# Products of no use in TensorE's waits inside the mLSTM recurrence of a two-block transformer step

## The chip, the cores and the metric

The kernel runs on one core of a Trainium2 chip. Its metric is the device time of one execution in microseconds (us), of which the median over several runs counts. TensorE's clock is granted at one of two levels, 1.2 and 2.4 GHz; in the profile 0.50 stands for the first and 1.00 for the second.

## The reference

Two transformer blocks are computed for 1024 tokens of width 1024, each with a mixer and a mixture of experts. The change touches one part of the first block: the mLSTM mixer, a recurrence over chunks of 128 tokens, run forward and backward, with four heads of 64 key and 128 value columns. For every chunk it needs the state left by the earlier chunks (`C_prev`) and the products inside the chunk:

```python
def _mlstm_chunk_outputs(q, k, v, log_i, log_f, prev):
    ...
    m_t = jnp.maximum(a, jnp.max(log_d, axis=-1))
    s = jnp.einsum('bhctk,bhcsk->bhcts', qc, kc) * jnp.exp(log_d - m_t[..., None])
    e_int = jnp.exp(a - m_t)
    num = (jnp.einsum('bhcts,bhcsv->bhctv', s, vc)
           + e_int[..., None] * jnp.einsum('bhcvk,bhctk->bhctv', C_prev, qc))
    den = jnp.sum(s, axis=-1) + e_int * jnp.einsum('bhck,bhctk->bhct', n_prev, qc)
    h = num / jnp.maximum(jnp.abs(den), jnp.exp(-m_t))[..., None]
```

## The kernel before

The program is a row of stages, each with its own instruction list for every engine; the engines meet only at semaphores. `stage_mlstm` holds the recurrence. Its unit of work is a pair, that is two heads of one direction in one chunk: 10 chunks (two of them context) by two directions by two pairs of heads make 40 pairs `p`. The first 8 belong to the context and give only a state; for the other 32, numbered `v` from 0, outputs are computed too. Two successive pairs, `v` even and `v` odd, are the four heads of one chunk and one direction. They share one set of decay factors, so one turn of the pattern is two pairs.

For a pair `v` TensorE does, in this order (lines of the kernel before):

- the inter product, queries by the state left by earlier chunks (L948), into columns 256 to 384 of two PSUM banks; the banks alternate with `v` (`out_banks`: banks 2 and 3, or 4 and 5);
- a wait until VectorE has finished the weights `pt` of this same pair `v` (`pt_ready`, v + 1);
- the scores of the next pair, keys by queries (L918), into banks 0 and 1;
- the value product, `pt` by the values (L954), into columns 0 to 128 of the same two banks as the inter product, with `start=True`, so that what stood there is overwritten;
- after an even `v`, the maxima for the next turn (L910), two products of 512 columns in the fp32r format;
- the local product, keys by weighted values (L966), from which VectorE makes the new state. It waits for GpSimd's `wv` and for VectorE to have read the one before.

VectorE does for each turn: `mask` (L1042, decay from the maxima), `weights` (L1051, `pt` = scores by decay) for the next pair, the sum of the inter and value products (L1063, `hsum`), four small operations for the denominator and the output (L1066 to L1077), and the new state (L1081). Beside them it has work of the convolution branch: a `reciprocal` of 128 columns for `v` 0 to 7 (L1090), and a product of 512 columns for `v` 12 to 19 (L1095). ScalarE exponentiates the decay factors, four operations ahead of odd `v`'s end (L977), scales the inter product (L995), squares finished outputs (L980), and takes one square root at `v` = 10 (L1005), with a change of activation table before and behind it. TensorE's order is the order in which the code is written; no planner is involved.

Of the kernel before, what the change touches and what calls it, by code (L numbers as in the profile page):

```python
# [31 lines left out]
KC = D_CONV // P  # L32
# [807 lines left out]
def stage_mlstm(s):  # L840
# [19 lines left out]
    with ExitStack() as stack:  # L860
# [5 lines left out]
        NM_high, NM_low = (sb(f"NM_{n}", [NCOL, P]) for n in ("high", "low"))  # L866
        NM4 = [sb(f"NM4_{n}", [NCOL, H1, P]) for n in ("high", "low")]
        R = lambda ap: ap.bitcast(F32R)
# [8 lines left out]
        out_banks = lambda v: 2 + 2 * (v % 2)  # L877

        with nc.Block() as block:
            @block.sync  # L880
            def _(sp):
                sp.wait_ge(zeros_set, 1)
                for i in range(2 * NT):
                    t, a = divmod(i, 2)
                    sp.dma_start(s.second_sum[t * P:(t + 1) * P, a * 512:(a + 1) * 512], zeros[:, :]).then_inc(zeros_stored, 16)
                sp.wait_ge(zeros_stored, 16 * 2 * NT)
# [18 lines left out]
            @block.tensor  # L905
            def _(pe):
                def maxima(g):

                    for i in range(2):
                        last = pe.matmul(s.bank[6].rearrange("p (h n) -> p h n", h=H1), R(group_of[:, NC * 2 + g:NC * 2 + g + 1]).to_broadcast([NCOL, P]),  # L910
                                         R(NM4[i][:, :, :]), start=(i == 0), stop=(i == 1))
                    last.then_inc(maxima_done, 1)

                def scores(v):
                    j, d, k = pairs[P0 + v]
                    t0 = tile_of(j, d) * P
                    for i in range(2):
                        last = pe.matmul(s.bank[i][:, 0:P], s.qkT[lanes(i), 2 + k, t0:t0 + P], s.qkT[lanes(i), k, t0:t0 + P],  # L918
                                         start=True, stop=True)
                    last.then_inc(scores_done, 1)  # L920

                for n, m in halves:
                    last = pe.matmul(s.bank[2 + n][:, :], s.ones[:, :], s.y[:, m, n * N:(n + 1) * N], start=(m == 0), stop=(m == KC - 1))
                    if m == KC - 1:
                        last.then_inc(mean_done, 1)
                for p, (j, d, k) in enumerate(pairs):
                    v = p - P0
                    if v in (-4, -3):
                        n = v + 4
                        for m in range(KC):  # L930
                            pe.wait_ge(squared, n * KC + m + 1)
                            last = pe.matmul(s.bank[4 + n][:, :], s.ones[:, :], sqy[:, m, n * N:(n + 1) * N], start=(m == 0), stop=(m == KC - 1))
                        last.then_inc(var_done, 1)
                    if v == 0:
                        pe.wait_ge(centred, 2 * KC)
                    if v == 1:
                        pe.wait_ge(var_read, 2)
                    if v == -1:
                        pe.wait_ge(maxima_set, 1)
                        maxima(0)  # L940
                        scores(0)
                    if v >= 0:
                        t0, bank = tile_of(j, d) * P, out_banks(v)
                        if v >= 2:
                            pe.wait_ge(combined, v - 1)
                        pe.wait_ge(state_moved, p - H1 + 1)
                        for i in range(2):
                            pe.matmul(s.bank[bank + i][:, 256:256 + W], s.qkT[lanes(i), k, t0:t0 + P], state[lanes(i), d, k, :],  # L948
                                      start=True, stop=True)
                        pe.wait_ge(pt_ready, v + 1)  # L950
                        if v + 1 < NV:
                            scores(v + 1)
                        for i in range(2):
                            last = pe.matmul(s.bank[bank + i][:, 0:W], pt[:, v % 2, i, :], s.v_aug[:, tile_of(j, d), 2 * k + i, :],  # L954
                                             start=True, stop=True)
                        last.then_inc(num_done, 1)
                        if v % 2 == 0 and v + 2 < NV:
                            pe.wait_ge(masked, v // 2 + 1)
                            maxima(v // 2 + 1)
                    if p < PS:  # L960
                        pe.wait_ge(wv_ready, 2 * (p + 1))
                        if p >= 1:
                            pe.wait_ge(state_moved, p)
                        for i in range(2):
                            h = 2 * k + i
                            last = pe.matmul(s.bank[7][lanes(i), 0:W], s.k_tok[:, tile_of(j, d), h * DK:(h + 1) * DK],  # L966
                                             wv[:, p % 2, i, :], start=True, stop=True)
                        last.then_inc(local_done, 1)
# [192 lines left out]
class OutNorm:  # L1161
# [47 lines left out]
    R = staticmethod(lambda ap: ap.bitcast(F32R))  # L1209
# [1535 lines left out]
class BlockEntry:  # L2745
# [44 lines left out]
    R = staticmethod(lambda ap: ap.bitcast(F32R))  # L2790
# [1360 lines left out]
```

## Time and profile before

| | us |
|---|---|
| median of 3 runs | 2859.05 |
| all runs | 2858.34, 2859.05, 2865.69 |
| the profiled execution | 2865.83 |
| its span, first to last instruction | 2864.1 |
| TensorE's mean granted clock over the span | 0.949 |
| TensorE busy | 2650.1 (93%) |
| VectorE busy | 1795.9 (63%) |
| ScalarE busy | 1294.6 (45%) |
| GpSimd busy | 1105.4 (39%) |

The recurrence proper, the 32 pairs with outputs, lies from about 423 us to 538 us after the span's start, 4% of it; most of the rest is the two expert stages. A matmul's busy time in this profile includes the time in which its last columns pass through the array, so matmuls that follow each other closely overlap: the distance from one start to the next is what one costs in a row. In a row of the timeline, "x4" means four instructions merged into one row, the number after the start is the time they take together, and the bracket at the end is the idle time of the engine ahead of them and what ended it. "issue" is idle time in which nothing that the profile shows was waited for.

### The profile page before, as it was taken

What the parts mean: (1) busy time and instruction counts of PE and PEld (TensorE: products, weight loads), DVE (VectorE), ACT (ScalarE), POOL (GpSimd) and SP (SyncE); (2) the same over time, 40 slices, a digit from 0 to 9 for tenths busy, and PEclk for the clock granted to TensorE, in tenths of its full rate; (3) what the DMA queues carried; (4) which work ended last, traced back from release to release, by engine and by line L of the source; (5) the groups of instructions that cost most, each with busy time, mean ns of one, the idle gap of its engine ahead of it and who ended that gap; (6) DMA issues with size and microseconds to landing.
All of it is one profiled execution on the core that took longest, in us unless ns stands there. A gap on an engine that the chain in (4) does not pass through costs nothing. (4 is left out here: it accounts for less than half of the span.)

```text
span 2864.1 us, 40780 instructions
## 1 busy us (share of the span) xinstructions
PE 2650.1 (93%) x12404; PEld 1987.1 (69%) x12405; DVE 1795.9 (63%) x2593; ACT 1294.6 (45%) x1816; POOL 1105.4 (39%) x1056
## 2 busy tenths in 40 slices
PE   6999989699899999999999977999999999877998
PEld 3455446486478888888888866875876877765786
DVE  3766767766677678678686657555544342557764
ACT  3320123632266567677675544146123232326653
POOL 1870023111666567567675540249201010005454
PEclk9999995699999999999999998999999999987999
DMA  8340010134288789999898866200311332428972
GB/s 296 133 154 1 30 59 1 68 128 187 82 305 294 249 291 323 306 328 316 265 353 296 259 162 207 73 1 2 62 45 52 103 88 66 171 110 312 323 225 43
DMA packets 187315, 484.59 MB, mean 169 GB/s; under 512 B 37484, under 2 KB 93344, under 8 KB 166456
## 3 DMA queue, kind: packets, MB, share of 16 engines
q1 hardware_dynamic: 143072, 372.83, 35.1%
q0 software_dynamic: 42592, 106.04, 15.5%
q10 hardware_dynamic: 1544, 4.33, 0.4%
q8 instruction: 62, 1.02, 0.2%
q14 instruction: 45, 0.37, 0.0%
HBM read 432.35 MB, written 95.69 MB: 184 GB/s over the span
## 5 line engine op out<-in xcount | busy, mean ns | idle before, releaser
L2219 PE MATMUL psum<-moe_high,moe_xg_high 128*128 128x512 f32 x960 | 390.0, 406 | 16.8 <-issue 16.7
L2221 PE MATMUL psum<-moe_high,moe_xg_low 128*128 128x512 f32 x960 | 378.0, 394 | 0.0
L2220 PE MATMUL psum<-moe_low,moe_xg_high 128*128 128x512 f32 x960 | 375.3, 391 | 0.0
L1633 DVE TENSOR_TENSOR moe_low<-moe_raw,moe_high 128x2048 fp32r<-128x2048 f32 x160 | 358.9, 2284 | 3.0 <-ACT moe_high L1617 1.5
L1617 ACT ACTIVATE moe_high<-moe_raw 128x2048 fp32r<-128x2048 f32 x160 | 297.9, 1920 | 11.0 <-DMA moe_raw<-in_w_e_up 8.3
L1609 POOL DMA_INDIRECT moe_landing<-moe_rows,moe_ig_now x124 | 225.9, 1822 | 109.4 <-POOL moe_ig_now L1606 91.4
L1606 POOL COPY moe_ig_now<-idx 128x1 int32 (+1 forms) x124 | 172.9, 1394 | 198.4 <-DVE moe_xg L1646 158.9
L2219 PEld LDWEIGHTS psum<-moe_high,moe_xg_high 128*128 128x128 f32 x960 | 181.7, 189 | 54.7 <-issue 20.5
L2206 PE MATMUL psum<-moe_high_down,moe_hid_high 128*128 x488 | 203.6, 417 | 8.9 <-DVE moe_hid_low L2297 8.6
L2221 PEld LDWEIGHTS psum<-moe_high,moe_xg_low 128*128 128x128 f32 x960 | 180.8, 188 | 42.9
L2220 PEld LDWEIGHTS psum<-moe_low,moe_xg_high 128*128 128x128 f32 x960 | 181.9, 190 | 36.0
L2252 ACT ACTIVATE moe_y_blk<-psum,row_w 128x1024 f32 x124 | 138.4, 1116 | 131.0 <-PE psum L2208 112.5
L2208 PE MATMUL psum<-moe_high_down,moe_hid_low 128*128 x488 | 192.2, 394 | 0.0
L2207 PE MATMUL psum<-moe_low,moe_hid_high 128*128 x488 | 192.1, 394 | 0.0
L590 DVE SCALAR_TENSOR_TENSOR conv_y<-upad,convw,conv_y 128x1024 f32<-128x1024 f32 x120 | 182.4, 1520 | 5.9 <-DVE x L621 1.7
L1633 DVE TENSOR_TENSOR moe_low<-moe_raw,moe_high_down 128x2048 fp32r<-128x2048 f32 x80 | 182.7, 2283 | 0.0
L1661 DVE TENSOR_TENSOR moe_xg_low<-psum,moe_xg_high 128x512 fp32r<-128x512 f32 x244 | 157.3, 686 | 27.0 <-ACT moe_xg_high L1656 26.5
L567 PE MATMUL psum<-hT,w_ring 128*128 128x512 f32 x384 | 169.0, 598 | 1.1 <-PEq L200 1.1
L2263 ACT ACTIVATE moe_silu<-psum 128x256 f32<-128x256 f32 x120 | 46.0, 383 | 272.7 <-PE psum L2221 272.7
L2302 DVE TENSOR_TENSOR moe_hid<-psum,moe_silu 128x256 f32<-128x256 f32 x120 | 50.4, 420 | 182.0 <-ACT moe_silu L2263 181.2
L1622 ACT ACTIVATE moe_high_down<-moe_raw 128x2048 fp32r<-128x2048 f32 x80 | 153.2, 1916 | 3.4 <-DMA moe_raw<-in_we_down 2.0
L1656 ACT ACTIVATE moe_xg_high<-psum 128x512 fp32r<-128x512 f32 x244 | 132.9, 597 | 15.1 <-PE psum L1650 8.9
(635 smaller groups left out, 5695.2 us busy)
## 6 DMA issues: line engine op xcount, KB each, us to landing
moe_raw<-in_we_gate SPq DMA_DIRECT2D x64, 1024.0 KB, 8.9
moe_raw<-in_we_up SPq DMA_DIRECT2D x64, 1024.0 KB, 12.6
moe_raw<-in_we_down SPq DMA_DIRECT2D x64, 1024.0 KB, 8.9
x<-in_w_ada POOLq DMA_DIRECT2D x16, 1024.0 KB, 5.6
x<-in_w_in SPq DMA_DIRECT2D x32, 512.0 KB, 6.4
moe_raw<-in_w_e_gate SPq DMA_DIRECT2D x16, 1024.0 KB, 9.6
moe_raw<-in_w_e_up SPq DMA_DIRECT2D x16, 1024.0 KB, 13.1
moe_raw<-in_w_e_down SPq DMA_DIRECT2D x16, 1024.0 KB, 9.9
```

Source lines behind the costliest of these rows:

```text
L567: last = pe.matmul(bank[:, 0:width], w[:, k, c0:c0 + P], h[:, k, :], start=(k == 0), stop=(k == KD - 1))
L590: c.link(dve, dve.scalar_tensor_tensor(to, rows, w, to, ALU.mult, ALU.add))
L1606: pool.tensor_copy(self.ig_now[q][:, :], idx[:, bass.ds(g + 2, 1)]).then_inc(self.ig_set, 1)
L1609: pool.indirect_dma_start(self.landing[:, q * D:(q + 1) * D], None, self.rows, bass.IndirectOffsetOnAxis(ap=self.ig_now[q][:, 0:1], axis=0 ...
L1617: act.activation(self.high[:, at:at + 2048].bitcast(F32R), self.raw[r][:, part], ACT.Copy).then_inc(self.w_high, 1)
L1633: dve.tensor_tensor(self.low[:, at:at + 2048].bitcast(F32R), self.raw[r][:, part], hi, ALU.subtract).then_inc(self.w_low, 1)
L2206: pe.matmul(by[n][:, :], R(hid_high[:, f, :]), w_hi, start=(f == 0), stop=False)
L2207: pe.matmul(by[n][:, :], R(hid_high[:, f, :]), w_lo, start=False, stop=False)
L2208: last = pe.matmul(by[n][:, :], R(hid_low[:, f, :]), w_hi, start=False, stop=(f == KF - 1))
L2219: pe.matmul(to, x_hi, R(of_k(w_hi, k)), start=(k == 0), stop=False)
L2220: pe.matmul(to, x_hi, R(of_k(w_lo, k)), start=False, stop=False)
L2221: last = pe.matmul(to, x_lo, R(of_k(w_hi, k)), start=False, stop=(k == KD - 1))
```

## The change

A function `keep_running` issues 8 matmuls for each of the pairs `v` = 0 to 7 and 4 for each later one, 8 x 8 + 24 x 4 = 160 in all, each with its own weight load. They stand between the inter product and the wait for `pt`. Each multiplies the 80 x 128 array `NM_high` by 256 columns of the 80 x 512 array `NM4[0]` in fp32r and writes columns 0 to 255 of the first of the pair's two banks. Nobody reads the result: the value product of the same pair overwrites columns 0 to 128, and columns 129 to 255 are never read. The inter product's columns start at 256 and stay as they are. No semaphore is added.

```diff
+                def keep_running(v):
+
+                    for _ in range(8 if v < 2 * KC else 4):
+                        pe.matmul(s.bank[out_banks(v)][:, 0:256].rearrange("p (h n) -> p h n", h=2), R(NM_high[:, :]), R(NM4[0][:, 0:2, :]), start=True, stop=True)
+
...
                         for i in range(2):
                             pe.matmul(s.bank[bank + i][:, 256:256 + W], s.qkT[lanes(i), k, t0:t0 + P], state[lanes(i), d, k, :],
                                       start=True, stop=True)
+                        keep_running(v)
                         pe.wait_ge(pt_ready, v + 1)
                         if v + 1 < NV:
                             scores(v + 1)
```

TensorE's instructions at the start of the recurrence, from the local product ahead of pair 0 to the inter product of pair 1, in the kernel before (`c_state` is the state, `qkT` queries and keys, `wv` the weighted values; a row is a matmul as written, before its passes):

```order
L966 MATMUL psum<-wv,k_tok 64x129 x2
L948 MATMUL psum<-c_state,qkT 128x129 x2
L918 MATMUL psum<-qkT 128x128 x2
L954 MATMUL psum<-v_aug,pt 128x129 x2
L910 MATMUL psum<-NM_high,group_of 128x512
L910 MATMUL psum<-NM_low,group_of 128x512
```

The same place in the changed kernel, whose lines are numbered 5 and 6 higher:

```order
L972 MATMUL psum<-wv,k_tok 64x129 x2
L953 MATMUL psum<-c_state,qkT 128x129 x2
L917 MATMUL psum<-NM_high 128x256 x8
L923 MATMUL psum<-qkT 128x128 x2
L960 MATMUL psum<-v_aug,pt 128x129 x2
L910 MATMUL psum<-NM_high,group_of 128x512
L910 MATMUL psum<-NM_low,group_of 128x512
```

Between the inter product and the next pair's scores there are now eight matmuls of 256 columns; the rest keeps its order, and so does every other engine's list.

## Rows read from the trace of the kernel before

**Rows 1.** Stretches of the recurrence: busy time (instructions) by engine, granted clock, DMA share, GB/s.
```profile
423.00:433.00 10.00, 6.90 (x58) 4.66 (x56) 6.91 (x20) 3.81 (x13) 4.74 (x8) 1.00 0.00 1
433.00:515.00 82.00, 76.45 (x372) 52.23 (x371) 62.04 (x203) 32.86 (x107) 26.53 (x44) 0.50 0.00 1
515.00:533.00 18.00, 11.37 (x90) 7.69 (x89) 13.62 (x48) 9.97 (x42) 2.40 (x4) 0.97 0.01 1
533.00:545.00 12.00, 3.90 (x16) 2.88 (x16) 5.60 (x23) 8.85 (x38) 0.00 (x0) 0.50 0.00 1
```

**Rows 2.** Waits from 422 to 540: total us, times, longest.
```profile
ACT inter L995 <- PE psum L954: 16.9, 15, 1.4
...
DVE c_state L1081 <- PE psum L966: 4.3, 2, 3.6
```

**Rows 3.** VectorE's timeline: two turns, at 1.2 and at 2.4 GHz.
```profile
505.11 0.69 DVE L1042 TENSOR_TENSOR decay<-psum,neg_mask 128x512 f32<-128x512 f32 x1
506.55 0.42 DVE L1051 TENSOR_TENSOR pt<-psum,decay 128x256 f32<-128x256 f32 x1 [0.76 <-ACT decay L977]
507.64 0.43 DVE L1063 TENSOR_TENSOR hsum<-psum,inter 128x258 f32<-128x258 f32 x1 [0.67 <-ACT inter L995]
...
511.67 0.68 DVE L1042 TENSOR_TENSOR decay<-psum,neg_mask 128x512 f32<-128x512 f32 x1
...
518.35 0.68 DVE L1042 TENSOR_TENSOR decay<-psum,neg_mask 128x512 f32<-128x512 f32 x1
...
524.89 0.68 DVE L1042 TENSOR_TENSOR decay<-psum,neg_mask 128x512 f32<-128x512 f32 x1
```

**Rows 4.** TensorE's timeline at 1.2 GHz, a turn of the first eight pairs.
```profile
447.55 0.80 PE L918 MATMUL psum<-qkT 64*128 64x128 f32 x4 [0.77 <-DVE pt L1051]
448.28 1.23 PE L954 MATMUL psum<-v_aug,pt 128*128 128x129 f32 x4
...
455.44 0.80 PE L918 MATMUL psum<-qkT 64*128 64x128 f32 x4 [0.78 <-DVE pt L1051]
```

**Rows 5.** ScalarE's timeline around the square root of pair 10.
```profile
464.51 0.63 ACT L995 ACTIVATE inter<-psum,EI 128x129 f32<-128x129 f32 x2 [1.42 <-PE psum L954]
465.16 1.28 ACT L1005 ACT_TABLE_LOAD   x1
...
468.83 1.28 ACT L977 ACTIVATE decay<-decay,E 128x128 f32<-128x128 f32 x4
```

**Rows 6.** VectorE's timeline at the same place, and at pair 31.
```profile
469.55 0.42 DVE L1051 TENSOR_TENSOR pt<-psum,decay 128x256 f32<-128x256 f32 x1 [1.98 <-ACT decay L977]
...
537.69 0.43 DVE L1063 TENSOR_TENSOR hsum<-psum,inter 128x258 f32<-128x258 f32 x1 [0.27 <-ACT inter L995]
```

**Rows 7.** TensorE's timeline at 2.4 GHz: inter product, wait, scores, value product.
```profile
429.58 0.49 PE L948 MATMUL psum<-c_state,qkT 64*128 64x129 f32 x4
431.71 0.49 PE L918 MATMUL psum<-qkT 64*128 64x128 f32 x4 [1.63 <-DVE pt L1051]
...
525.49 0.49 PE L948 MATMUL psum<-c_state,qkT 64*128 64x129 f32 x4
526.81 0.49 PE L918 MATMUL psum<-qkT 64*128 64x128 f32 x4 [0.83 <-DVE pt L1051]
527.23 0.71 PE L954 MATMUL psum<-v_aug,pt 128*128 128x129 f32 x4
```

**Rows 8.** TensorE's timeline in the output projection: fp32r products of 512 columns.
```profile
569.57 0.60 PE L1259 MATMUL psum<-out_w_high,out_src_high 128*128 128x512 f32 x1 [4.76 <-DVE out_w_low L1432]
569.98 0.63 PE L1260 MATMUL psum<-out_w_low,out_src_high 128*128 128x512 f32 x1
...
573.32 0.39 PE L1259 MATMUL psum<-out_w_high,out_src_high 128*128 128x512 f32 x1
573.55 0.40 PE L1260 MATMUL psum<-out_w_low,out_src_high 128*128 128x512 f32 x1
```

**Rows 9.** One line's weight loads: count, ns min/median/max, first and last start, shape.
```profile
L3857 PEld LDWEIGHTS psum<-h_high,gw_high x256: 186/188/189, 2168.9 to 2432.3; 128*128 128x128 f32 x128
```

## The prediction

> **What bounds the kernel now.** I read the page first for where the recurrence lies and how large it is: 115 us of 2864. Then the stretches of that part, with the clock [rows 1]. TensorE's clock was granted at 2.4 GHz until 433 us, stood at 1.2 GHz from 433 to 515 us, rose, and fell again near 533 us. In the 82 us at 1.2 GHz TensorE was busy for 76.45 us, 93%; that looks like a stretch bounded by TensorE at half its clock, and if it were, giving the clock back would be worth tens of us. So the question is whether anybody waits for TensorE there.
>
> The waits answer it [rows 2]. VectorE waited for TensorE's local product 4.3 us, in two waits, one of them 3.6 us long, so it is nothing that comes back in every turn. ScalarE waited for the value product 16.9 us over 15 waits, but what counts is whether VectorE then waited for ScalarE because of it. VectorE's timeline shows a turn of two pairs [rows 3]: the mask, then 0.76 us idle until ScalarE has exponentiated enough of the decay factors, the weights, then 0.67 us idle until ScalarE's `inter` is there. That `inter` belongs to the odd pair; ScalarE runs it only behind its four exponentials, so it is late because of them and not because of a value product. Otherwise VectorE works without a break. The loop is VectorE's work plus those two waits for ScalarE, 1.43 us a turn, in which TensorE has no part.
>
> The trace holds a direct test. From mask to mask the turn at 1.2 GHz took 511.67 - 505.11 = 6.56 us, and the turn at 2.4 GHz took 524.89 - 518.35 = 6.54 us [rows 3], with the same work on VectorE. Twice the clock brought 0.02 us. The turn between the two, in which the clock rose, took 6.68 us, with no gain in it either.
>
> **The change part by part.** It adds 160 fp32r matmuls of 256 columns. It removes nothing and moves no other instruction, on any engine. It has two effects: they take TensorE's time, and they may hold the clock at 2.4 GHz.
>
> Price of one at 2.4 GHz. The trace has no fp32r product of 256 columns in the recurrence. The nearest row is of 512 columns: start to start 573.55 - 573.32 = 0.23 us [rows 8]. Columns stream at a constant rate, so I take half, 0.115 us; four are 0.46 us and eight 0.92 us. The upper end is 0.23 us, if the halved columns gain nothing because something else sets the pace: 0.92 and 1.84 us. The lower end is zero, which is what a product costs that is hidden whole.
>
> Weight loads. In a row of such products a weight load lasts 0.188 us [rows 9] though the products start 0.23 us apart, so it lies beside the product before it. The Trainium skill (TensorE: Matmul & The Clock Gate, Part 3, "What overlaps and what doesn't") says that weight loads overlap products in flight only when the row group differs, which speaks against this change, since all the added products use the same rows. This trace does not bear it out: the products of the projection share all 128 rows and still stand 0.23 us apart. By the rule one added product would cost some 0.115 + 0.188 = 0.30 us, eight 2.4 us; by the row it is 0.115 us.
>
> What hides them. Ahead of the scores of an even turn half, TensorE was idle at 2.4 GHz for 1.63 us in the first eight pairs and for 0.83 us in the later ones, until `pt` was there [rows 7]. In the odd half `pt` is ready and there is no such wait, so those products push TensorE's list back until the next wait takes them up. The two halves together bring 2 x 0.92 = 1.84 us against 1.63, and 2 x 0.46 = 0.92 against 0.83: TensorE would be 0.21 or 0.09 us late at the scores. That is covered too. The scores and value product took 448.28 - 447.55 + 1.23 = 1.96 us at 1.2 GHz [rows 4] and 527.23 - 526.81 + 0.71 = 1.13 us at 2.4 GHz [rows 7]. With the former VectorE did not wait for them, so at the higher clock there is 0.83 us to spare. Cost on the path: 0. At the upper price the lateness would be 3.68 - 1.63 - 0.83 = 1.22 us in each of four turns, and 1.84 - 0.83 - 0.83 = 0.18 us in each of twelve, 7.0 us together. GpSimd is not reached: its `wv` waits for the local product, and the turn has room for it while VectorE sets the pace. The two engines behind TensorE that could feel it are ScalarE (`inter`) and VectorE (the new state), both covered by the same 0.83 us.
>
> What the higher clock gives, if it holds. Two places only. At pair 10 ScalarE runs `inter`, waits 1.42 us for the value product ahead of it, and then goes without a break through a table load, the square root and another table load to the exponentials at 468.83 us [rows 5]; VectorE waited 1.98 us for them, where the other turns wait 0.76 us [rows 6, 3]. The value product comes 0.83 us sooner, and 1.98 - 0.83 = 1.15 us is still above 0.76 us, so all of it counts: -0.8 us. Behind the last pair VectorE waited 0.27 us for ScalarE [rows 6], whose value product at 2.4 GHz is 1.23 - 0.71 = 0.52 us shorter; VectorE is then bound by its own work, so -0.27 us, rounded -0.3. Everything else in the turn is VectorE's and ScalarE's: 0. Behind pair 31 there are no added products and TensorE has little to do until 545 us, 3.90 us in 12 [rows 1], so the stage behind starts at 1.2 GHz as before.
>
> Sum: -0.8 - 0.3 + 0 = -1.1 us. The profiled execution took 2865.83 us (span 2864.1, and 1.7 around it), so its like would take 2864.7 us. It was 0.24% above the median of the runs, 2859.05 us; the same difference gives 2858.0 us, a change of 0.04%. What a measurement of this kernel can tell from no change is about 0.3%, 8.6 us.
>
> **The rivals.**
>
> B, the clock is at 1.2 GHz all the same, and the added products land on the path. This is the case on the other side. For it: TensorE was busy for 93% of 82 us and the clock did not rise [rows 1], so being busy by this count is not enough. The Trainium skill (TensorE: Matmul & The Clock Gate, Part 1) says that the half clock is the default and that sustained work releases it within microseconds; the stretch from 433 us does not agree, since there 76 us of work did not. Against B: the clock held from 515 to 533 us with TensorE busy for only 11.37 of 18 us, and the fall at 433 us came behind a wait of 1.63 us [rows 7], which the added products now fill. And the kind of product that is added is one that raises the clock: in the projection they went from 0.41 us apart to 0.23 in the 3.75 us from the first one, which followed an idle time of 4.76 us [rows 8]. The price: an added product at 1.2 GHz costs half of 569.98 - 569.57 = 0.41 us, 0.2 us. A turn of the first eight pairs had 0.77 us idle in its 7.89 us [rows 4], so 16 x 0.2 - 0.77 = +2.4 us in each of four turns, and with no idle time at all 8 x 0.2 = +1.6 us in each of twelve: +9.7 + 19.7 = +29 us, 2888 us. Where it rises on the way, as the added work itself should make it do, half of that: 2874 us. It decides from the point where 30% of the recurrence runs at 1.2 GHz, since 0.3 x 29 is 8.7 us.
>
> C, the clock holds but the products cost more than half of a 512-column one, by the weight load or a slow start behind each fp32 product. Against it rows 8 and 9, for it that neither shows this very shape. The upper price gives +7.0 - 1.1 = +5.9 us, 2865 us.
>
> D, TensorE is on the path after all. ScalarE's 16.9 us of waits for the value product [rows 2] speak for it. If every one of the some 12 turns at the lower clock gained the 0.83 us, it would be -10 us, 2849 us. The two turns of equal length at the two clocks [rows 3] speak against it.
>
> **How the numbers follow.** A, the forecast, 0.76: no change. B 0.12, of which 0.08 is long enough to be slower by over 0.3%. C 0.06, within 0.3%. D 0.06, of which 0.05 counts as faster. Slower: 0.08 and 0.02 for a set of runs as far off as the highest of before (2865.69), 0.10. Faster 0.05. Same 0.85. The range runs from 2851 us, near D, to 2871 us, the lighter part of B; A alone would lie between 2855 and 2865, by the spread of the runs before.
>
> **What would show it.** In the profile after, the granted clock from 433 to 515 us reads 1.00 if the first effect is right, and 0.50 if B is. The added products stand about 0.115 us apart. The turns of VectorE keep their lengths, 6.5 us where nothing of the convolution lies in them and 7.9 us in the first eight pairs; its wait of 1.98 us shrinks to about 1.15 us and the 0.27 us at pair 31 goes. The recurrence ends about 1 us sooner. If turns at 2.4 GHz are shorter than those at 1.2 GHz were by more than 0.1 us, D is right and the forecast wrong. If VectorE waits for ScalarE's `inter` after an even pair, and ScalarE for the value product, the products are too long for their room.

## The result, and the profile after

| | before | after |
|---|---|---|
| median us (4 runs each) | 2862.24 | 2897.89 |
| lowest and highest us | 2858.34, 2865.69 | 2892.24, 2899.31 |
| profiled span us | 2864.1 | 2897.6 |
| mean granted clock over the span | 0.949 | 0.945 |

The kernel before has four runs here, one more (2865.42 us) than ahead of the prediction; one slow execution of it, of 8841.69 us, is left out everywhere. The change made the kernel slower: the ratio after to before is 1.0119, 95% interval 1.0104 to 1.0135. The forecast was no change, 2858 us, with a range up to 2871; it is wrong. The sign that the prediction named for its rival B, a granted clock of 0.50 between 433 and 515 us, is there from 441 us on.

The stretches of the recurrence after the change (columns as in [rows 1]):

```profile
423.00:433.00 10.00, 9.23 (x70) 6.97 (x72) 7.04 (x22) 4.06 (x14) 3.30 (x6) 1.00 0.01 2
433.00:441.00 8.00, 6.70 (x54) 4.99 (x53) 6.30 (x20) 2.41 (x8) 2.39 (x4) 1.00 0.00 0
441.00:515.00 74.00, 74.00 (x326) 52.75 (x322) 44.69 (x141) 22.32 (x63) 18.07 (x30) 0.50 0.00 1
515.00:570.00 55.00, 54.33 (x235) 38.66 (x234) 28.98 (x98) 22.20 (x92) 8.55 (x14) 0.50 0.00 1
```

The clock held for 8 us longer than before and then fell all the same. From 441 us to the end of the recurrence it stood at 1.2 GHz, and TensorE was busy for 128.3 of 129 us, waiting for nobody: now it is TensorE that sets the pace. TensorE's timeline there, a turn of the later pairs from scores to scores:

```profile
463.06 0.80 PE L953 MATMUL psum<-c_state,qkT 64*128 64x129 f32 x4
463.79 1.22 PE L917 MATMUL psum<-NM_high 80*128 80x256 f32 x4
464.94 0.80 PE L923 MATMUL psum<-qkT 64*128 64x128 f32 x4
465.67 1.23 PE L960 MATMUL psum<-v_aug,pt 128*128 128x129 f32 x4
...
472.71 0.80 PE L953 MATMUL psum<-c_state,qkT 64*128 64x129 f32 x4
473.44 1.22 PE L917 MATMUL psum<-NM_high 80*128 80x256 f32 x4
474.60 0.80 PE L923 MATMUL psum<-qkT 64*128 64x128 f32 x4
```

A turn is 474.60 - 464.94 = 9.66 us without a wait. In the kernel before, TensorE's list went round at 1.2 GHz like this, from scores that started right behind `pt` (506.55 + 0.42 = 506.97 us [rows 3]) and with no bracket, so no wait, behind them:

```profile
507.03 0.80 PE L918 MATMUL psum<-qkT 64*128 64x128 f32 x4
...
510.40 0.80 PE L948 MATMUL psum<-c_state,qkT 64*128 64x129 f32 x4
510.99 0.64 PE L918 MATMUL psum<-qkT 64*128 64x128 f32 x4
...
513.94 0.64 PE L918 MATMUL psum<-qkT 64*128 64x128 f32 x4
```

That is 513.94 - 507.03 = 6.91 us. The difference of 2.75 us comes apart as follows. From the start of the inter product to the scores it is 464.94 - 463.06 = 1.88 us now and was 510.99 - 510.40 = 0.59 us: 1.29 us, twice a turn. Of these, 1.15 us are the four products, and 0.14 us come because the next product now starts 0.73 us behind the inter product, where the scores started 0.59 us behind it. The scores of the odd half, which followed the inter product directly, took 0.57 us to the value product (511.56 in the timeline) and take 0.73 us now (465.67 - 464.94): 0.16 us. 2 x 1.29 + 0.16 = 2.74 us.

VectorE's timeline shows who waits now:

```profile
503.41 0.68 DVE L1048 TENSOR_TENSOR decay<-psum,neg_mask 128x512 f32<-128x512 f32 x1
504.85 0.42 DVE L1057 TENSOR_TENSOR pt<-psum,decay 128x256 f32<-128x256 f32 x1 [0.76 <-ACT decay L983]
506.21 0.43 DVE L1069 TENSOR_TENSOR hsum<-psum,inter 128x258 f32<-128x258 f32 x1 [0.93 <-ACT inter L1001]
...
510.61 0.43 DVE L1069 TENSOR_TENSOR hsum<-psum,inter 128x258 f32<-128x258 f32 x1 [1.32 <-ACT inter L1001]
513.06 0.68 DVE L1048 TENSOR_TENSOR decay<-psum,neg_mask 128x512 f32<-128x512 f32 x1
```

The wait of 0.76 us is the old one [rows 3]; the wait of 1.32 us behind the even pair did not exist. It is the sign named in the prediction for "the products are too long for their room". The waits say the same. In the kernel before, from 422 to 540 us:

```profile
DVE hsum L1063 <- ACT inter L995: 11.0, 17, 0.7
```

And after, from 422 to 580 us (the first row to be compared with [rows 2]):

```profile
ACT inter L1001 <- PE psum L960: 54.7, 26, 4.5
...
DVE hsum L1069 <- ACT inter L1001: 34.9, 30, 1.3
```

Where the 33.5 us of span are: the first mask came 1.5 us sooner (422.01 for 423.52), the 15 turns from the first to the sixteenth mask took 138.46 us for 107.66 (+30.8), the tail behind it to the last `hsum` 9.55 us for 6.51 (+3.0), and 1.2 us lie elsewhere in the kernel.

### The profile page after: what moved, and what is told of

It reads as the page before. It is cut to its first block and busy times, and to the rows that moved or that the text cites. A ratio compares the mean times of both kernels' runs of the same rounds, so it can differ in the third digit from the quotient of the medians.

```text
span 2897.6 us, 41100 instructions
## 1 busy us (share of the span) xinstructions
PE 2692.0 (93%) x12564; PEld 2020.7 (70%) x12565; DVE 1798.5 (62%) x2593; ACT 1295.6 (45%) x1816; POOL 1107.8 (38%) x1056
## 3 DMA queue, kind: packets, MB, share of 16 engines
q8 instruction: 63, 1.03, 0.1%
```

## The experiments

Single runs of this kernel scatter: the kernel before alone ranged from 2855.55 to 2867.16 us over the chips used. So the length of the recurrence is compared inside the profiles, as the distance from the first to the sixteenth mask on VectorE (15 turns), with TensorE's mean granted clock over it. The time column is one run beside one run of the kernel before on the same chip; where it gives a ratio, both kernels have several runs. In the second column "8 / 4" means 8 products for a pair of the first eight and 4 for a later one, and "behind the maxima" is the place of TensorE's second wait, explained below.

| run | products: pairs, place | rows | 15 turns us | clock | time against before |
|---|---|---|---|---|---|
| before | none | | 107.66 | 0.62 | |
| after | 8 / 4, every pair | 80 | 138.46 | 0.57 | ratio 1.0119 (1.0104 to 1.0135) |
| half | 4 / 2, every pair | 80 | 126.82 | 0.57 | 2882.3 for 2867.2 |
| even_only | 8 / 4, even pairs | 80 | 120.59 | 0.55 | 2875.0 for 2867.2 |
| double | 16 / 8, every pair | 80 | 131.86 | 0.78 | 2888.8 for 2867.2 |
| full_rows | 8 / 4, every pair | 128 | 118.43 | 0.82 | 2873.8 for 2867.2 |
| full_rows_8 | 8 / 8, every pair | 128 | 110.05 | 0.95 | 2864.2 for 2861.2 |
| second_wait_only | 5, behind the maxima | 128 | 107.98 | 0.83 | 2870.2 for 2861.2 |
| two_waits_80 | 8 / 4 even, 5 behind the maxima | 80 | 117.25 | 0.77 | 2871.2 for 2861.2 |
| two_waits | the same | 128 | 107.26 | 0.95 | 2862.3 for 2861.2 |
| two_waits_t | the same kernel again | 128 | 107.93 | 0.95 | ratio 0.9997 (0.9983 to 1.0010) |
| reordered | none, other engines' order | | 118.42 | 0.51 | ratio 1.0037 (1.0022 to 1.0053) |
| reordered_filled | as two_waits | 128 | 96.07 | 0.98 | ratio 0.9963 (0.9950 to 0.9975) |

**Number and place at the low clock.** All edits are to the changed kernel.

```diff
-                    for _ in range(8 if v < 2 * KC else 4):
+                    for _ in range(4 if v < 2 * KC else 2):
```

> Half the added products: 4 for each of pairs 0 to 7, 2 for each later one. Theory 1 (the clock is at 1.2 GHz and the added products lie on TensorE's list, which sets the pace): four cost 1.15 us a pair in the changed kernel and eight 2.00, so two fewer save 0.42 us a pair and 0.85 us a turn; turns of pairs 8 and later 8.8 us instead of 9.65, turns of the first eight about 9.65 instead of 10.1 to 11.4; about 18 us over the kernel before. Theory 2 (the products disturb another engine's accesses, or the mere presence of the wait structure costs): less than proportional, above 27 us. Theory 3 (the clock rises once the stream is denser): 2.4 GHz from some point on, within 5 us of before.

The clock fell in the first eight pairs again and stayed down. TensorE's timeline from one even pair's scores to the next even pair's:

```profile
499.94 0.80 PE L923 MATMUL psum<-qkT 64*128 64x128 f32 x4
...
508.74 0.80 PE L923 MATMUL psum<-qkT 64*128 64x128 f32 x4
```

One turn, 8.80 us, as theory 1 said. The 15 turns took 19.2 us more than before and the single run 15.1 us, where 18 was expected. The one turn with four products a pair that lay wholly at 1.2 GHz took 8.42 us, not the 9.65 expected.

```diff
-                    for _ in range(8 if v < 2 * KC else 4):
+                    for _ in range((8 if v < 2 * KC else 4) if v % 2 == 0 else 0):
```

> The added products only ahead of the even pairs, where TensorE waited for the weights in the kernel before; none ahead of the odd ones. Theory 1 (1.2 GHz, TensorE's list sets the pace): a turn of later pairs is TensorE's 6.91 us of before (scores at 507.03 to scores at 513.94) plus 1.3, 8.2 us; the first eight 9.1 us; about +15 us over the kernel before. If the place had been the fault and the wait hid them: +0 to +3 us. If the clock holds: -1 us.

```profile
502.19 0.64 PE L923 MATMUL psum<-qkT 64*128 64x128 f32 x4
...
510.39 0.64 PE L923 MATMUL psum<-qkT 64*128 64x128 f32 x4
```

8.20 us, again as theory 1 has it; +12.9 us over 15 turns and +7.8 us in the single run, where 15 was expected. So the place ahead of the even pairs is no shelter at 1.2 GHz: what was a wait of 0.83 us at 2.4 GHz was none in the kernel before's turn of 6.56 us, and at most 0.64 us in its turns of 7.2 to 7.8 us. The rival that the products disturb another engine falls: with place and number varied, the turn follows TensorE's list.

```diff
-                    for _ in range(8 if v < 2 * KC else 4):
+                    for _ in range(16 if v < 2 * KC else 8):
```

> Twice the added products: 16 for each of pairs 0 to 7, 8 for each later one. If the clock stays at 2.4 GHz when TensorE's stream is dense enough (the amount decides): turns of 6.5 us in the later pairs, at most 8.5 us in the first eight, within 4 us of the kernel before. If it stays at 1.2 GHz whatever is added: turns of about 11.4 us and 14.8 us, about 33 + 30 = 60 to 65 us over the kernel before.

Neither case alone. The clock held until 494 us, with turns of 8.4 us in the first eight pairs (7.9 before) and 6.4 to 7.8 us behind them, and then fell; once it was low throughout, the turn was 11.4 us (530.04 - 518.68 at the masks) and nothing raised it again. With twice the amount the clock held longer, in this one execution, and it did not come back.

**Rows of the array.** `full` is a new 128 x 256 array, which VectorE fills once from the convolution's output. The edit changes the values of the operands together with their rows; no run tells the two apart.

```diff
+        full = sb("full", [P, 256])
...
-                        pe.matmul(..., R(NM_high[:, :]), R(NM4[0][:, 0:2, :]), start=True, stop=True)
+                        pe.matmul(s.bank[out_banks(v)][:, 0:256], R(full[:, 0:128]), R(full[:, :]), start=True, stop=True)
```

> The same number of added products, 256 columns in fp32r, but over all 128 rows of the array instead of 80 (their operands are a copy of 256 columns of the convolution's output; nobody reads the result). If the thinness of the added products keeps the clock down: 2.4 GHz through the recurrence, turns of 6.5 and 7.9 us, about 1 us under the kernel before. If rows make no difference: as the changed kernel, turns of 9.65 us and +34 us.

The clock fell at 445.25 us, and this time rose again, at 448.70 us; it fell for good at 496.45 us, in the stretch with four products a pair. TensorE's timeline at the first fall and rise (a value product takes 0.71 us at 2.4 GHz and 1.23 at 1.2):

```profile
443.58 0.40 PE L911 MATMUL psum<-NM_low,group_of 80*128 80x512 f32 x1
444.93 0.44 PE L973 MATMUL psum<-wv,k_tok 128*64 128x129 f32 x4 [0.94 <-DVE c_state L1089]
445.30 0.80 PE L954 MATMUL psum<-c_state,qkT 64*128 64x129 f32 x4
446.03 2.08 PE L918 MATMUL psum<-full 128*128 128x256 f32 x8
448.03 0.80 PE L924 MATMUL psum<-qkT 64*128 64x128 f32 x4
448.76 0.71 PE L961 MATMUL psum<-v_aug,pt 128*128 128x129 f32 x4
```

The 48 us at 2.4 GHz behind this are the test of the gain that the prediction put on the clock. VectorE's turn with the square root:

```profile
461.85 0.68 DVE L1050 TENSOR_TENSOR decay<-psum,neg_mask 128x512 f32<-128x512 f32 x1
463.56 0.42 DVE L1059 TENSOR_TENSOR pt<-psum,decay 128x256 f32<-128x256 f32 x1 [1.03 <-ACT decay L984]
...
469.14 0.68 DVE L1050 TENSOR_TENSOR decay<-psum,neg_mask 128x512 f32<-128x512 f32 x1
```

7.29 us where the kernel before took 8.12 (466.88 to 475.00): 0.83 us less, the term as forecast (the wait of 1.98 us is 1.03 us now). The turn ahead of it took 6.42 us, as it did within 0.01 us in every run at the high clock with the old order, where it had taken 6.28, so 0.69 us of the gain is left. The next four turns took 7.48, 7.61, 7.75 and 7.15 us; before, at 1.2 GHz, they took 7.53, 7.67, 7.75 and 7.16. Rival D, that TensorE is on the path of every turn at 1.2 GHz, falls.

> Full-row products in the place of the changed kernel, 8 for every pair instead of 8 and then 4. Eight full-row ones raised the clock again within 3 us of its fall (445.3 to 448.8), four did not in 45 us, and eight of 80 rows did not in 60 us. If that is a property of the amount and the rows: the clock may fall but rises again each time, at 2.4 GHz for nine tenths of the recurrence; turns of 7.9 and 6.6 us with some of 9, and +0 to +6 us against the kernel before. If it was chance: it stays low once fallen, turns of 11.4 us, as in the run with twice the number, +20 us.

The edit is `range(8)` in place of the two numbers. The clock was low from 439 to 449 us and then high to the end: 2.4 us more than before over 15 turns, one of which took 10.2 us, the one at the low clock. So it did rise again, but after 10.3 us and not after 3.5 as in full_rows. The turn with the square root took 7.70 us for full_rows' 7.29: with eight products a pair about half of the gain there is used up, so even at 2.4 GHz their cost on the path is not 0 everywhere. Behind pair 31 VectorE did not wait for `inter` here, where it waited 0.27 us before [rows 6]; the last two `hsum` stood 1.71 us apart for 1.94.

**Both waits of TensorE.** In six of the eight falls within the 15 turns of the runs up to here the clock went at TensorE's other wait of the turn, the one behind the maxima for VectorE's new state, 0.94 to 1.09 us long: within 0.3 us behind its end in the changed kernel (441.00 us), half (440.20), full_rows (445.25) and full_rows_8 (438.75), and inside it in double (494.15) and at the second fall of full_rows (496.45). Two do not fit. In the kernel before, the clock fell at 433.20 us, which is before that wait began (432.92 + 0.40 = 433.32) and 1.5 us behind the end of the wait of 1.63 us; the 434.26 us of the expectation below is the first slow product, not the fall. In even_only it fell at 435.90 us, where a wait of 0.66 us for the odd pair's state began. And waits in the same place passed without a fall: 0.77 us in the changed kernel (432.89), 1.09 us in the kernel before (522.95). In the changed kernel:

```profile
439.43 0.40 PE L910 MATMUL psum<-NM_low,group_of 80*128 80x512 f32 x1
440.79 0.47 PE L972 MATMUL psum<-wv,k_tok 128*64 128x129 f32 x4 [0.96 <-DVE c_state L1087]
441.19 0.80 PE L953 MATMUL psum<-c_state,qkT 64*128 64x129 f32 x4
```

So products were put there too, behind a wait until VectorE has summed the pair that used the banks before. The diff is against the changed kernel and leaves out the operands, which are those of full_rows.

```diff
-                def keep_running(v):
+                def keep_running(v, n):
...
-                        keep_running(v)
+                        keep_running(v, (8 if v < 2 * KC else 4) if v % 2 == 0 else 0)
...
                             maxima(v // 2 + 1)
+                            if p < PS:
+                                pe.wait_ge(combined, v)
+                                keep_running(v + 1, 5)
```

> Full-row products put into both of the waits that TensorE has at 2.4 GHz: 8 or 4 ahead of the even pairs' scores as in the run for even pairs, and 5 more (0.7 us at 2.4 GHz) behind the maxima, ahead of the local product that waits for VectorE's state; none ahead of the odd pairs. In every trace so far the clock fell at the end of the wait behind the maxima (434.26 before, 441.19 after, 445.30 and 496.59 with full rows, 494.20 with twice the number), which none of them filled. Theory 4 (an unfilled wait of about 1 us with the maxima and value product ahead of it is what lets the clock go): 2.4 GHz from 423 to 538 us, turns 7.9 and 6.5 us, and then the terms of the forecast: -0.8 -0.3, so 1 us under the kernel before and not more. Theory 5 (the clock falls by chance or by the total amount of work): it falls again somewhere, turns of TensorE's list behind it of about 6.9 + 1.3 + 1.3 = 9.5 us, +5 to +30 us.

107.26 us for 15 turns, clock 0.95 over them. The turns are those of VectorE, 7.9 us in the first eight pairs. The clock still fell three times, at 450.30, 474.20 and 532.20 us, and the first two times it was back after 6.9 and 3.5 us. None of these falls came behind the maxima, so theory 4 is not the whole of it. But waits were left: the first fall came at the end of one of 0.65 us for the odd pair's state, the second 0.4 us behind one of 0.77 us that four products do not fill.

> As the run before it in this list, with the 80-row operands of the changed kernel instead of the full-row ones. If only the place of the products counts: 2.4 GHz throughout, -1 us. If the rows count as well: the clock falls in the first eight pairs as in the changed kernel (441 us), and does not rise again; turns of about 9.5 us, +25 to +30 us.

The same with 80 rows: the clock fell at 439.20 us, with products in both waits (0.50 us was left of the one ahead of the scores),

```profile
438.93 0.49 PE L923 MATMUL psum<-qkT 64*128 64x128 f32 x4 [0.50 <-DVE pt L1060]
439.35 1.23 PE L960 MATMUL psum<-v_aug,pt 128*128 128x129 f32 x4
```

and it came back only at 493.85 us, to hold beyond the last mask. Theory 4 falls: the clock goes without a wait of about 1 us behind the maxima. So does my "does not rise again". That some wait is needed for a fall is not ruled out, since no run of this order has every wait filled. The turns at the low clock were 8.4 to 9.9 us.

> Full-row products only behind the maxima, 5 a turn; nothing ahead of the scores. Theory 4, in the form that this one wait decides: the clock holds, -1 us. If both waits have to be filled: it falls in the first eight pairs, where the wait ahead of the scores is 1.63 us; then turns of 6.91 + 1.3 = 8.2 us for the later pairs, +12 us at the most, less where it rises again.

The clock fell eight times and seven times rose again, after 3.5 to 6.9 us; it was 0.83 on average, and the 15 turns took 107.98 us, as before. This is the smallest number of full-row products tried, 5 a turn, and it gains nothing either. The run's time is 9 us over that of before with a recurrence of the same length; that difference lies outside it and is within what single runs of this kernel show.

> The run with both waits filled once more, timed in rounds against the kernel before. Its one look had 107.3 us from the first to the last mask where the kernel before had 107.7, with the clock at 2.4 GHz for all but some microseconds. Expected: same as before within 0.3%, ratio between 0.998 and 1.001; the clock is worth the 0.8 us at the square root and nothing else while VectorE sets the pace.

0.9997 (0.9983 to 1.0010), over ten runs: no change. That is what the prediction forecast for a clock that holds, and here it was 0.95 over the 15 turns, with two short falls (481 and 502 us).

**Taking the pace away from VectorE.** ScalarE now scales the odd pair's inter product ahead of the four exponentials, and VectorE makes the next weights behind the odd pair's denominator.

```diff
                 for v in range(NV):
                     j, d, k = pairs[P0 + v]
-                    if v % 2 == 1 and v + 1 < NV:
-                        exps(v // 2 + 1)
                     act.wait_ge(num_done, v + 1)
...
                                        scale=s.EI[:, j, d, h:h + 1]).then_inc(inter_ready, 1)
+                    if v % 2 == 1 and v + 1 < NV:
+                        exps(v // 2 + 1)
...
-                    if 0 <= v + 1 < NV:
+                    if 0 <= v + 1 < NV and (v < 0 or v % 2 == 0):
                         weights(v + 1)
...
                         c.link(dve, dve.reciprocal(D2[:, :, 1:2], D2[:, :, 0:1]))
+                        if v % 2 == 1 and v + 1 < NV:
+                            weights(v + 1)
```

> The kernel before without any added product, but with the two waits of VectorE for ScalarE (0.76 + 0.67 us a turn) covered: ScalarE scales the odd pair's inter product ahead of the four exponentials, and VectorE sums it behind the mask, ahead of the next weights. If those waits set the pace (the reading of the prediction) and TensorE comes next, a turn falls to the larger of VectorE's own work (5.1 to 6.5 us) and TensorE's list, 6.91 us at 1.2 GHz: with the clock low 107.7 - 15 x 6.91 = 4 us less, with the clock high up to 15 x 1.43 = 21 us less. Expected in between and by the clock: -4 to -10 us. If VectorE did not set the pace: no change.

Slower, by 0.37%, against an expectation of 4 to 10 us less. The clock stood at 1.2 GHz for all but a few microseconds, and the turn became a ring through three engines: 448.13 - 440.14 = 7.99 us. Its closing part:

```profile
445.93 0.63 ACT L993 ACTIVATE inter<-psum,EI 128x129 f32<-128x129 f32 x2 [3.17 <-PE psum L954]
...
446.59 0.43 DVE L1063 TENSOR_TENSOR hsum<-psum,inter 128x258 f32<-128x258 f32 x1 [0.60 <-ACT inter L993]
...
447.65 0.42 DVE L1051 TENSOR_TENSOR pt<-psum,decay 128x256 f32<-128x256 f32 x1
...
448.13 0.80 PE L918 MATMUL psum<-qkT 64*128 64x128 f32 x4 [0.87 <-DVE pt L1051]
```

The odd value product frees ScalarE's `inter`, that frees `hsum`, and behind it come the weights for which TensorE waits 0.87 us: TensorE's whole list and this wait lie one behind the other, 7.12 + 0.87 us. I had counted the list alone, 6.91 us.

> The reordered kernel with the full-row products in both waits. TensorE is the next in line there, so its clock should now count: 2.4 GHz held, turns of 5.5 to 6.5 us, -13 to -21 us against the kernel before and 5 us or more under the reordered kernel without the products. If the products no longer find waits to stand in (13 of them are 1.9 us of TensorE's time a turn, 9 are 1.3), they cost what they bring and it is within 3 us of the reordered kernel.

With the clock at 0.98 the same order takes 96.07 us for 15 turns, 6.1 to 6.5 us for most, and the kernel is faster than before: 0.9963 (0.9950 to 0.9975), some 10 us, which is less than the 13 expected. Against the reordered kernel the products are worth 2874.5 - 2853.2 = 21 us. This is the one place in which products of no use paid, and the best kernel of the study. No run has the new order at 2.4 GHz without products, so what the clock alone would bring there is not known.

## Why the prediction was wrong

**What bounds the kernel before** was read rightly. VectorE and its waits for ScalarE set the turn [rows 3]: with the clock at 0.62, 0.83 and 0.95 over the 15 turns they took 107.66, 107.98 and 107.26 us, and the ratio of the last kernel was 0.9997. But the direct test of the prediction, 6.56 us at 1.2 GHz against 6.54 at 2.4, hides how little room was left. In that low turn TensorE's list took 6.91 us, so TensorE fell 0.35 us behind; the scores that had followed `pt` at once at 507.03 us came 0.42 us late at 513.94 (513.10 + 0.42 = 513.52), and at 515.15 us the clock rose. Had it stayed low, TensorE would have gone on losing some 0.35 us in each of the three turns behind, an estimate from these rows. At 1.2 GHz, then, whatever is added to TensorE's list in the short turns is late by its whole length.

**The value of the clock** was right in its places. At the square root it was 0.83 us as forecast, of which the turn ahead took 0.14 back. The 0.27 us at pair 31 went where the clock was still high there (full_rows_8, 0.23 us between the last two `hsum`), but not in two_waits, where it had fallen at 532 us and the wait was 0.40 us. Over the 15 turns two_waits was 0.4 us shorter and two_waits_t 0.3 us longer than before, so the sum of -1.1 us itself is not shown by any whole run.

**The step that failed** is "Cost on the path: 0", and in it the case that the clock holds, to which A gave 0.76. It rested on three things [rows 1, 7, 8]: the clock had survived 18 us with TensorE busy for 11.37, the fall at 433 us stood behind a long wait ahead of the scores, and fp32r products raise the clock in the projection. The runs showed in its place that the clock went at 441.00 us with that wait down to 0.34 us, and that from there the products lay on a TensorE list of 9.66 us that had no wait left to hide them. The fall came 0.2 us behind the wait behind the maxima, which the products did not cover, but that this wait was its cause is not shown: covering most of it with 80-row products did not keep the clock either. The projection's products, 128 rows and in an unbroken row, were no measure for 80 rows in small groups. The long wait ahead of the scores was not right behind the fall of the kernel before either: it ended at 431.71 us, the clock fell at 433.20. I had the contrary evidence in hand, 76 us of work at 1.2 GHz [rows 1], and gave B 0.12.

**Rival B** is what happened. Its price of 29 us was near the 33.5 of the span by luck, since two errors offset (and its second term should be 12 x 1.6 = 19.2, not 19.7). It had the clock low from the first turn, +9.7 us for the first four, which in fact took 2.4 us more, because the clock held until 441 us and the first three took 22.26 us for 22.16. And it put a product at 1.2 GHz at 0.2 us, half of a 512-column one of the projection. It costs 2.00 / 8 = 0.25 us in eights and 1.15 / 4 = 0.29 us in fours, start to start, and another 0.44 us a turn (2 x 0.14 + 0.16) because other products now stand behind the inter products and ahead of the odd half's scores; so the eleven later turns took 28.5 us more. A nearer row than the projection's was at hand, the maxima of the recurrence itself, fp32r, with the same 80 rows and 512 columns, at 2.4 and at 1.2 GHz in the kernel before:

```profile
432.60 0.48 PE L910 MATMUL psum<-NM_high,group_of 80*128 80x512 f32 x1
432.92 0.40 PE L910 MATMUL psum<-NM_low,group_of 80*128 80x512 f32 x1
...
441.27 0.78 PE L910 MATMUL psum<-NM_high,group_of 80*128 80x512 f32 x1
441.84 0.63 PE L910 MATMUL psum<-NM_low,group_of 80*128 80x512 f32 x1
```

They stand 0.32 and 0.57 us apart; half of that, 0.16 and 0.29 us, is close to what the added ones cost.

**The price at 2.4 GHz** was 0.14 us (426.38 to 427.52 for eight) where I took 0.115; the first three turns, at 7.90 us for 7.95 and 7.89 in the second and third, had room for it, so rival C did not come up.

**The range** left B's full case outside. With a rival that has one outcome, at a price worked out at 2888 us, and a mechanism whose trigger I could not derive from any row, 0.12 was too little.

What stays open is what decides the moment at which the clock falls or rises. Full rows, more products, and products in both waits each went with a shorter low time, but 80-row products rose once (494 us in two_waits_80) and full rows once did not (496 us in full_rows). No run here separates the row count from chance by repetition, nor from the values of the operands: the profiles are one execution each, except that the mean clock over the span was alike in all four runs of the changed kernel (0.943 to 0.947) and in all ten of two_waits_t (0.964 to 0.968).

## What to carry to other kernels

Work that is meant to hold the clock must be paid for at the low clock as well as at the high one, since that is when it is least hidden: price it on the engine's whole list at 1.2 GHz before adding it, with the start-to-start distance of the nearest product of the same rows. Compare that list with the turn: two turns of equal length at the two clocks show who sets the pace, not how much room is left. Ask first who sets the pace: while another engine did, 2.4 GHz was worth at most 0.8 us in 108; only when that engine's waits had been taken out were the products and the clock together worth 21. And an order that looks shorter by one engine's idle time can close a ring through three engines, so count the ring and not the longest list.

## What the runs showed of the hardware

- TensorE busy for 128.3 of 129 us, without a wait, stayed at 1.2 GHz throughout (changed kernel, 441 to 570 us). The kernel before, with no product added and waits in between, rose at 515.15 us, after 82 us.
- Products of 80 rows, in any number tried, left it there for 54 us or more (439.20 to 493.85 us in two_waits_80; in the others to the end of the recurrence). Eight of 128 rows a pair were followed by a rise after 3.5 us (full_rows, 445.25 to 448.70) and 10.3 us (full_rows_8), five behind the maxima after 3.5 to 6.9 us, seven times (second_wait_only); four a pair by none from 496.45 us to the end of the recurrence (full_rows).
- The clock fell with TensorE busy between waits of less than 1 us: the last two before the fall were 0.34 and 0.96 us in the changed kernel, 0.95 and 0.18 us in even_only. A wait of 1.09 us in the kernel before (522.95) brought no fall.
- A group of products of one kind between two others costs more than itself: in the changed kernel the product behind each inter product starts 0.73 us behind it, where the scores had started 0.59 us behind it, and the value product 0.73 us behind the odd half's scores for 0.57; 0.44 us a turn.
